# A two-network forward pass on one core: router, expert entry and exit reordered, scores in row pairs

## What is computed

```python
def diff_attend(q, k, v, lam):            # 8 heads, 2 maps m of width 64 each
    s = jnp.einsum('bhmqd,bhmkd->bhmqk', q, k).astype(jnp.float32) * DH_D ** -0.5
    p = jax.nn.softmax(s, axis=-1)
    a = p[:, :, 0] - lam * p[:, :, 1]
    return jnp.einsum('bhqk,bhkd->bhqd', a.astype(v.dtype), v)

def moe_ffn(u, router_w, router_b, w1, b1, w2, b2):
    ...
    logits = (xf @ router_w + router_b).astype(jnp.float32)
    top_val, top_idx = lax.top_k(logits, TOP_K)
    gate = jax.nn.softmax(top_val, axis=-1).astype(u.dtype)
    ...
    def expert_block(args):
        tok, e = args
        hcat = xf[tok] @ w1[e] + b1[e]
        h_glu = jnp.minimum(hcat[:, :D_FF], SWIGLU_LIMIT)
        h_lin = jnp.clip(hcat[:, D_FF:], -SWIGLU_LIMIT, SWIGLU_LIMIT)
        act = h_glu * jax.nn.sigmoid(SWIGLU_ALPHA * h_glu) * (h_lin + 1)
        return act @ w2[e] + b2[e]
```

## Time and profile before

| | us |
|---|---|
| median of 3 runs (2755.54 to 2761.25) | 2755.63 |
| the profiled execution | 2757.8 |
| its span, first to last instruction | 2755.9 |
| TensorE busy in the span | 2460.0 (89%) |
| VectorE / ScalarE / GpSimd busy | 762.0 / 553.6 / 38.8 |
| mean granted TensorE clock | 0.948 of full |
| expert weights: issues of 1 MB, arena and ring | 222 + 162 |

### The profile page before, as it was taken

How to read it: one execution, slowest core, us unless ns; L and a number is a source line. 1 busy time by engine, 2 the same in 40 slices (tenths; PEclk the granted TensorE clock), 3 DMA queues, 4 the chain that set the end, 5 groups by cost and what they waited for, 6 DMA issues and landing times. The chain is left out here.

```text
span 2755.9 us, 36442 instructions
## 1 busy us (share of the span) xinstructions
PE 2460.0 (89%) x15176; PEld 1632.7 (59%) x15176; DVE 762.0 (28%) x1853; ACT 553.6 (20%) x1374; POOL 38.8 (1%) x50
## 2 busy tenths in 40 slices
PE   6999978997978887979887767999999999999998
PEld 4785746686433333423332225877887788678887
DVE  1010345432111110111111003642440325624431
ACT  2110112411111111211111013441110211512110
POOL 0000001000000000000000000100000000100000
PEclk9999999998999998999899888999999999999999
DMA  7132242144699999899999994323333333123432
GB/s 313 63 135 77 95 155 89 60 172 170 255 421 420 407 420 421 326 420 420 421 420 421 421 421 174 121 75 109 139 133 125 134 142 138 46 77 122 153 121 78
DMA packets 86934, 608.35 MB, mean 221 GB/s; under 512 B 9552, under 2 KB 11728, under 8 KB 16080
## 3 DMA queue, kind: packets, MB, share of 16 engines
q1 hardware_dynamic: 86224, 602.49, 55.3%
q0 software_dynamic: 400, 2.46, 0.2%
q10 hardware_dynamic: 144, 1.05, 0.1%
HBM read 604.91 MB, written 1.05 MB: 220 GB/s over the span
## 5 line engine op out<-in xcount | busy, mean ns | idle before, releaser
L500 PE MATMUL bank<-arena,ring 128*128 128x272 f32 (+3 forms) x3200 | 761.7, 400 | 8.2 <-ACT arena L839 4.1
L500 PEld LDWEIGHTS bank<-arena,ring 128*128 128x128 f32 x3200 | 609.7, 191 | 154.1 <-issue 54.5
L2208 PE MATMUL bank<-arena 128*32 128x512 f32 x2184 | 281.0, 632 | 53.2 <-DMA arena<-in_w_e 53.2
L530 PE MATMUL bank<-arena,ring 128*128 128x272 f32 (+2 forms) x1216 | 281.2, 391 | 6.0 <-DVE arena L1666 6.0
L530 PEld LDWEIGHTS bank<-arena,ring 128*128 128x128 f32 x1216 | 233.9, 193 | 49.2 <-DVE arena L1666 6.9
L1542 DVE TENSOR_TENSOR arena<-bank,arena 128x256 f32<-128x256 f32 x56 | 23.8, 424 | 825.3 <-PE bank L2187 825.3
L2208 PE MATMUL bank<-ring,arena 128*32 128x512 f32 x1400 | 180.1, 624 | 49.6 <-DMA ring<-in_w_e 49.3
L2208 PEld LDWEIGHTS bank<-arena 128*32 128x32 f32 x2184 | 60.8, 112 | 214.5 <-DMA arena<-in_w_e 110.8
L1652 DVE SCALAR_TENSOR_TENSOR arena<-arena,par 128x272 f32<-128x272 f32 (+1 forms) x296 | 148.8, 503 | 10.5
L2225 PE MATMUL bank<-arena 128*32 128x256 f32 x1824 | 121.6, 411 | 28.7 <-DMA arena<-in_w_e 26.5
L990 ACT ACTIVATE arena<-bank 32x256 f32<-32x256 f32 x224 | 83.9, 374 | 252.2 <-PE bank L2225 249.8
(11 more groups left out here) (394 smaller groups left out, 2209.0 us busy)
## 6 DMA issues: line engine op xcount, KB each, us to landing
arena<-in_w_e SPq DMA_DIRECT2D x222, 1024.0 KB, 25.9
ring<-in_w_e SPq DMA_DIRECT2D x162, 1024.0 KB, 25.9
ring<-in_w_up SPq DMA_DIRECT2D x44, 1024.0 KB, 4.8
ring<-in_w_l SPq DMA_DIRECT2D x37, 1024.0 KB, 4.8
ring<-in_w_ada SPq DMA_DIRECT2D x24, 1024.0 KB, 6.3
ring<-in_w_proj SPq DMA_DIRECT2D x24, 1024.0 KB, 4.8
ring<-in_w_down SPq DMA_DIRECT2D x32, 704.0 KB, 4.0
...
```

What stands on the lines that cost most here:

```text
L500: mm = pe.matmul(o[:, a:n], ring[:, s, k * 256 + c * P:k * 256 + (c + 1) * P], rhs(k), start=(k == 0), stop=(k == KT - 1))
L530: mm = pe.matmul(o[:, a:n], ring[:, s, k * P:(k + 1) * P], rhs(part * kt + k), start=(part == 0 and k == 0), stop=(part == parts - 1 and k ...
L2208: mm = pe.matmul(bank[q * GROUP:(q + 1) * GROUP, 4 + g % 2, :], xe[:, (g // CHUNK) % 2, k, s:s + GROUP], w[:, q * 512:(q + 1) * 512], star ...
```

## The change

**Scores.** `qz` and GpSimd's copies are gone. The two maps of one query tile are two products over 64 rows each, one on the upper and one on the lower half of the array, into two banks; TensorE waits for two probabilities before each pair. The buffers of `PA`, `den` and `rden` are renumbered to 2 * qt + m.

**Router.** Barrier 5 is gone. ScalarE squares each tile of x as VectorE finishes it, and `x_sum` puts the norm's sum for tile c - 1 behind the output product c. The logits are taken k by k as u2 comes, ahead of the turning. The bias products are taken out of the router: the gates are turned directly after the expert order. GpSimd fetches the bias rows into other places and later (`b2r` behind `merged`, `b1r` behind the norm's root).

**Expert entry.** Barrier 6 is gone. Gathers 1 to 3 stand between the steps of item 0. The 16 turns of the first bias stand in item 1, four behind each of its first four steps; the 8 products of the second bias stand in item 2, one behind each step. ScalarE copies the turned bias in iteration 1, and VectorE waits for that copy there. The load of `most` stands in iteration 2.

**Expert exit.** Barriers 7 and 8 are gone, except inside the unused pass. The last gates are turned inside the last `w2`, into bank 6. The last `scatter` counts after each bank, and VectorE adds bank by bank. TensorE's branch stands directly behind the last `scatter`.

**Tables.** `sqrt_table` takes a root of one constant, so that the table is loaded then: after the gates' sigmoids, after the experts, and at the head of each `result_tiles`.

The diff, cut to its core:

```diff
@@ more_barrier @@
+        def more_barrier(eng, n):
+            eng.drain().then_inc(sem("more_phase"), 1)
+            eng.wait_ge(sem("more_phase"), 3 * n)
...
@@ ScalarE @@
-            for c in range(8):
-                tile_skip(at, c % 2 == 1)
-            phase(act, 5)
-
-            norm_squares(act, lambda k: xT[:, k, :], lambda k: sq2[:, k, :])
+            def sqrt_table():
+                act.activation(lamc[:, 6:7], cst("eps"), ACT.Sqrt)
+
+            sqrt_table()
+            act.wait_ge(sem("merged"), 1)
+            for k in range(KT):
+                tile_taken(act, at, k % 2 == 1)
+                act.activation(sq2[:, k, :], xT[:, k, :], ACT.Square).then_inc(sem("squares"), 1)
...
+                if n == 1:
+                    act.wait_ge(sem("bias_step"), 1)
+                    act.activation(b1P[:, :, :], bank[:, 7, :].rearrange("p (a b) -> p a b", a=2 * KT), ACT.Copy)\
+                       .then_inc(sem("pgT_ready"), 1)
...
             def result_tiles(parts, g, a=0):
 
+                sqrt_table()
...
@@ VectorE @@
+                if n == 1:
+                    dve.wait_ge(sem("pgT_ready"), 2)
...
-            phase(dve, 8)
             for k in range(KT):
+                dve.wait_ge(sem("scattered"), k // 2 + 1)
...
@@ TensorE @@
             def d_scores(h):
-                for j in range(4):
-                    m, qt = j // 2, j % 2
+                for qt in range(2):
                     if h >= 1:
-                        pe.wait_ge(sem("probs"), 4 * h + j - 3)
-                    pe.matmul(bank[:, j, :], qz[m][:, h, qt * P:(qt + 1) * P], kd[:, h, :],
-                              start=True, stop=True).then_inc(sem("scores"), 1)
+                        pe.wait_ge(sem("probs"), 4 * h + 2 * qt - 2)
+                    for m in range(2):
+                        pe.matmul(bank[:, 2 * qt + m, :], qd[64 * m:64 * m + 64, h, qt * P:(qt + 1) * P],
+                                  kd[64 * m:64 * m + 64, h, :], start=True, stop=True).then_inc(sem("scores"), 1)
...
-            project(pe, at, 4, lambda k: y1[:, k, :], T)
-            phase(pe, 5)
-
-            norm_sums(pe, at, lambda k: sq2[:, k, :], T)
-            pe.wait_ge(sem("u2_ready"), KT)
+            project(pe, at, 4, lambda k: y1[:, k, :], T, behind=lambda c: x_sum(c - 1) if c >= 1 else None)
+            x_sum(KT - 1)
+            at.norm += KT
+            for k in range(KT):
+                pe.wait_ge(sem("u2_ready"), k + 1)
+                for t in range(TT):
+                    mm = pe.matmul(bank[:, 4, t * NE:(t + 1) * NE], u2T[:, k, t * P:(t + 1) * P], wr[:, k, :],
+                                   start=(k == 0 and t == 0), stop=(k == KT - 1), skip_group_check=True)
...
             pe.wait_ge(sem("sel_ready"), 1)
-            for b in range(4):
-                gather(0, b, 6 + b % 2)
+            pe.wait_ge(sem("most_known"), 1)
+            gather(0, 0, 6)
             for n in range(NI + 2):
                 before = ITEMS[n - 1][1] if 1 <= n <= NI else []
                 quad, chunk = quad_due(n), chunk_due(n)
+                if n == 1:
+                    pe.wait_ge(sem("bias_loaded"), 32)
+                    pe.wait_ge(sem("xe_ready"), 4)
+                if n == 2:
+                    pe.wait_ge(sem("bias_loaded"), 32)
+                    pe.wait_ge(sem("u2tok_ready"), 2 * TT)
+                    most = pe.value_load(most_i[0:1, 0:1], min_val=0, max_val=T)
                 for k in range(KT):
+                    if n == 0 and k % 2 == 0 and k < 6:
+                        gather(0, k // 2 + 1, 7 if k % 4 == 0 else 6)
                     if n < NI:
                         w1_step(n, k)
+                    if n == 1 and k < 4:
+                        turn_b1(k)
+                    if n == 2:
+                        add_b2(k)
...
-            phase(pe, 7)
-            most = pe.value_load(most_i[0:1, 0:1], min_val=0, max_val=T)
             with pe.If(most > 0):
...
-            phase(pe, 8)
```

149 lines of the change are left out of this document (83 added, 66 removed).

## The result

| | before | after |
|---|---|---|
| median of 5 executions each, us | 2755.63 | 2736.03 |
| lowest to highest | 2754.03 to 2761.25 | 2726.50 to 2738.40 |
| profiled execution | 2757.8 | 2726.5 |
| span | 2755.9 | 2724.7 |
| mean granted TensorE clock | 0.948 | 0.956 |

What follows compares the result with a forecast made beforehand. TensorE was taken to bound the attention, step latency the router and exit, and DMA the expert stream. Terms summed to 35.6 us off 2757.8 (profiled), giving 2722.2, or 2720.0 against the median; range 2712 to 2731.

Steps and rivals of the forecast that it cites:

- scores in row pairs: Differential attention: two half-row score products run at once, a full factor of two; 9.4 us less, bounds 0 to 11.
- norm sums between products: Ahead of the router: six of eight norm sums move ahead of the last output product; 0.65 us less.
- logits first: Router: logits follow the shifts, ending about 7.5 us after the root, turnings behind them; 5.95 us less.
- biases out of the entry: Expert entry: both bias products no longer hold up gates and gather, 4.05 and 5.25 us; 9.3 us less.
- entry gives back: Expert entry: shape changes cost 0.6 us and the weight stream stands about 2.3 us; 2.9 us lost, bounds 0 to 6.
- exit: Expert exit: earlier scatter, TensorE's branch hidden beside it, norm sums at once at full clock; 10.6 us less, bounds 3.5 to 11.
- tables: Norm roots: ScalarE's table loaded early in idle time, saving 0.88 us at each of three norms; 2.6 us less.
- a microsecond taken from the attention, the router or the exit counts once: Stretches outside the expert weight stream: time saved there shortens the kernel fully; time saved inside the stream counts nothing.
- Row pairs without overlap: Attention scores: half-row products run one after the other at their old 0.43 us each; 2729.4 us, chance 0.14.
- The branch not hidden: Expert exit: TensorE's branch waits for its queue or fetches only afterwards; 6.5 us back, 2726.5 us, chance 0.14.
- Stream dry for longer: Expert items 1 and 2: low clock makes the weight stream stand 10 to 12 us longer; 2731 us, chance 0.08.
- Slower: Attention: half-row products leave TensorE at 1.2 GHz, a head takes 16.4 us; 52 us lost, 2772 us, chance 0.03.

Runs made afterwards that it cites:

- e4_before_more: The kernel before the change, with products nobody reads added in TensorE's waits, laid for its own waits; median 2740.77 us, ratio 0.9943.

## Why the prediction was wrong, step by step

In us. "At the place" is read in the traces; "free" is what the medians of the executions show when the part alone is undone in the changed kernel or made in the one before; "held" is read with the added products, in the traces for the parts and in the medians for the whole. A figure in the column "free" is uncertain by 4 to 6 us either way, except that of the whole.

| step | forecast | at the place | free | held |
|---|---|---|---|---|
| scores in row pairs | 9.4 | 8.4 | 1 (undone), 7 (alone) | 8.4 |
| norm sums between products | 0.65 | 0.5 (117.91 to 117.37) | | |
| logits first | 5.95 | 3.0 | -1.5 | 3.6 to 4.5 |
| biases out of the entry | 9.3 | 8.95 | 4.9 (both) | |
| entry gives back | -2.9 | -3.0 | | |
| exit | 10.6 | 10.6, 10.8, 9.1 | 8.5 | |
| tables | 2.6 | 0.88 a norm | -1.6 | 2.65 |
| whole change | 35.6 | 31.2 (first traces) | 22 | 34 to 38 |

**What held.** The row pairs overlap; GpSimd, VectorE and ScalarE didn't take over. The biases cost what rows 5 said, and the stream stops for 3 us behind the eighth issue. The tables held with the clock up (2.65 us of 2.6). The exit's chain held, but that its 11.7 us came so near to 11.5 in the first trace is partly luck: the scatter took 5.21 us and not 6.11, and the branch stuck out by 1.14 us and not at all. In the third trace, with the scatter at full clock, it is 13.2.

**The step that failed first: the size of the steps at TensorE's clock.** The sum took a duration from a row and put it at another place as it stood. I took the logits at 0.125 us each, 4.00 for 32. These rows stand behind turnings, at full clock. In the changed kernel the logits stand first behind the idle time of the norm and pay for the low stretch that the turnings had paid for, and it costs the logits more (7.04 us in place of 4.00) than the turnings (3.2 in place of 1.8). The logits' end came 2.9 us later behind the root than forecast (10.4 and not 7.5). It is not the whole of the 5 us by which the first release came late: the router's root itself was 2.8 us late (649.2 where the forecast's terms give 655.85 - 9.4 = 646.4), mostly by the low stretch at 563, and from the root to the release 44.8 us passed where the terms give 42.6.

**The step that failed most: "a microsecond taken from the attention, the router or the exit counts once".** It counts once at its place, and then the low stretches of the clock fall on other work. The places themselves gave 28 to 31 us up to the exit's root, of 33.0 forecast. Behind it the forecast had 2.6 us more, and the two typical traces of the changed kernel lost 4 to 10, with 69 and 75 us at half clock where the kernel before had 59 and 49. With the clock held up nothing of the kind is lost: the rest behind the exit's root takes 1057.5 us in `e4_before_more` and 1051.9 to 1055.4 in the changed kernels of that set, and the change as a whole is worth 34 to 38 us. The single parts show it less well. The pairs lose 3.0 of their 8.4 us right behind the heads, and keep them with the clock held; but what the executions say of pairs, order and tables alone (1, -1.5 and -1.6 us) isn't told from the forecast's sizes for the pairs and the tables, nor from nothing. The forecast knew the low clock only as a price for half-row products and for the biases, at one place each; it had no rival in which the clock takes back a gain elsewhere.

**The base.** The first trace of before had 3.7 us more between two roots than the second, and the first of the changed kernel was its luckiest. Their difference, 31.2, looked like the forecast; the medians differ by 22. One trace of each would have confirmed a wrong sum.

**Rivals.** Row pairs without overlap: refuted. The branch not hidden: half true. It is longer (6.2 us) than the 4.39 of rows 8 and sticks out 1.1 us behind a scatter mostly at half clock, 2.5 behind one at full clock. Stream dry for longer: no, 2.8 us. Slower: no.

What stays open is what decides whether a low stretch lasts 6.8 or 17 us behind the same 2.96 us of idle time: both traces show the same work there. Nor is it shown why the changed kernel, without added products, meets more time at half clock behind the exit than the kernel before. Without added products the traces with the early tables take 837.7 to 844.0 us from the fifth root on and those without them 836.1, but the executions without them are no faster.

## What to carry to other kernels

Where TensorE waits and then works, the first thing behind the wait can run at half clock (in two of three traces behind the 3.0 us at 561, in all three behind the 3.4 us ahead of the logits); when work is reordered, ask what now stands there, and take its duration at that clock. Hold the clock up in such waits (here 2733.8 to 2702.5 us, more than the whole reordering gave). Size small edits in traces, stage by stage, between stretches at the same clock: with the clock free a gain of some microseconds can be lost anywhere in the program, and medians of five executions don't resolve it, with the added products either. Judge the whole by the medians of several sets, and read at least two traces of each kernel before putting a sum against them.
